# Second experts of a two-block transformer kernel: two accumulation arrays in DRAM, four places for gate and up weights, loops over twelve experts

## The reference, cut to what matters

```python
N_EXPERTS_2 = 64
TOP_K = 6
# per expert e, for the tokens that chose it (rows h of the normalised input):
#   hid = silu(h @ w_exp_gate_2[e]) * (h @ w_exp_up_2[e]) * gate_weight      1024 -> 256
#   out[token] += hid @ w_exp_down_2[e]                                      256 -> 1024
# x = x + gate_m * (shared_expert(h) + sum over experts)
# result: rms_norm(x, g_final_2)
```

## Time and profile before

| | |
|---|---|
| three runs | 1967.75, 1969.74, 1974.19 us, median 1969.74 |
| the profiled execution | 1969.31 us, of which its span is 1967.3 us |
| mean granted TensorE clock in it | 0.960 |
| experts' gate and up products of the second block | from 1248 to 1921 us of the span |
| end of the experts to end of the span | 46 us |

### The profile page before, as it was taken

One profiled execution on the slowest core, in us unless ns is written; L12 is line 12 of the kernel. 1 busy time (PEld: TensorE's weight loads), 2 busy tenths in 40 slices (PEclk: granted clock), 3 DMA queues, 4 the chain that ended last, 5 costly groups with the idle time before them and its releaser, 6 DMA issues. The chain is left out here.

```text
span 1967.3 us, 24773 instructions
## 1 busy us (share of the span) xinstructions
PE 1793.4 (91%) x7962; PEld 1157.1 (59%) x7962; DVE 1007.1 (51%) x1976; ACT 781.6 (40%) x1404; POOL 559.0 (28%) x435
## 2 busy tenths in 40 slices
PE   6989999989989959999999699899999999999992
PEld 3434447754333327776788575577766766666661
DVE  1766416431111136632633344677777776767673
ACT  2411226311110135633632122566655555555551
POOL 4997707011111118901100000222322222222321
PEclk9889999989999979999999799999999999999996
DMA  5353410658999953322022444599999999999973
GB/s 192 129 181 107 171 43 4 253 190 358 407 404 397 359 179 110 106 86 91 1 86 90 163 177 160 186 343 340 348 325 327 333 328 337 329 326 325 320 262 108
DMA packets 116829, 441.71 MB, mean 225 GB/s; under 512 B 27428, under 2 KB 31924, under 8 KB 79368
## 3 DMA queue, kind: packets, MB, share of 16 engines
q1 hardware_dynamic: 93672, 406.94, 54.8%
q0 software_dynamic: 23040, 33.64, 7.4%
q10 hardware_dynamic: 32, 0.04, 0.0%
HBM read 438.34 MB, written 55.11 MB: 251 GB/s over the span
## 5 line engine op out<-in xcount | busy, mean ns | idle before, releaser
L1882 DVE TENSOR_TENSOR big_parts<-big,h_cols_parts 128x1024 fp32r<-128x1024 f32 x256 | 305.7, 1222 | 47.2 <-ACT h_cols_parts L1935 41.2
L2146 POOL DMA_INDIRECT acc_scratch<-heads,small x80 | 131.5, 1644 | 529.4 <-DVE small L1913 296.8
L1935 ACT ACTIVATE h_cols_parts<-big 128x1024 fp32r<-128x1024 f32 x256 | 262.8, 1059 | 27.9 <-PE bank L1841 23.2
L1872 PE MATMUL bank<-big,heads 128*128 128x512 f32 x512 | 235.2, 602 | 0.8 <-ACT heads L1943 0.8
L1839 PE MATMUL bank<-h_cols_parts,heads_parts 128*128 128x512 f32 x512 | 206.2, 403 | 2.2 <-DVE heads_parts L1902 2.2
L1841 PE MATMUL bank<-h_cols_parts,heads_parts 128*128 128x512 f32 x512 | 200.8, 392 | 0.0
L1840 PE MATMUL bank<-big_parts,heads_parts 128*128 128x512 f32 x512 | 200.0, 391 | 0.0
L1872 PEld LDWEIGHTS bank<-big,heads 128*128 128x128 f32 x512 | 92.1, 190 | 92.8 <-issue 91.8
L458 PE MATMUL bank<-big,h_cols 128*128 128x512 f32 x320 | 144.1, 605 | 0.3 <-ACT heads L608 0.3
L1968 ACT ACTIVATE heads<-bank 128x512 f32<-128x512 f32 x64 | 38.3, 598 | 239.5 <-DMA acc_scratch<-heads,small 213.5
L1517 PE MATMUL bank<-big,heads 128*64 128x512 f32 x512 | 118.5, 617 | 14.7 <-DMA big<-in_w_exp_up_dram 13.9
(11 more groups left out here) (438 smaller groups left out, 3335.2 us busy)
## 6 DMA issues: line engine op xcount, KB each, us to landing
big<-in_w_exp_gate_dram SPq DMA_DIRECT2D x96, 1024.0 KB, 13.4
big<-in_w_exp_up_dram SPq DMA_DIRECT2D x96, 1024.0 KB, 20.5
big<-in_w_exp_down_dram SPq DMA_DIRECT2D x72, 1024.0 KB, 22.8
big<-in_w_in_dram SPq DMA_DIRECT2D x13, 2048.0 KB, 8.7
x_res<-in_w_exp_down_dram SPq DMA_DIRECT2D x16, 1024.0 KB, 25.0
junk<-in_w_mod_dram SPq DMA_DIRECT2D x12, 1024.0 KB, 5.1
spare<-in_w_mod_dram SPq DMA_DIRECT2D x12, 1024.0 KB, 6.4
big<-in_w_out_dram SPq DMA_DIRECT2D x4, 2048.0 KB, 9.1
```

Of the source, the lines that this page charges most:

```text
L1872: mm = pe.matmul(b_y[half][:, :], hidt[:, b, P * j:P * j + P], dn[q][:, j, 512 * half:512 * half + 512], start=j == 0, stop=j == FH - 1)
L1882: dve.tensor_tensor(gu_low[q][:, :, part, :], gu[q][:, :, part, :], gu_high[:, :, part, :].bitcast(F32), ALU.subtract).then_inc(w_low, 1)
L1935: act.activation(gu_high[:, :, part, :], gu[q][:, :, part, :], ACT.Copy).then_inc(w_high, 1)
L2146: return pool.indirect_dma_start(out=K.acc_dram, out_offset=bass.IndirectOffsetOnAxis(at, 0), in_=rows, in_offset=None, bounds_check=S - 1 ...
```

## The change

- Even experts' scatters add into an array of their own in DRAM, `even_dram`, odd ones into `acc_dram` as before. Each has its own semaphore. The scatter of expert i-1 waits for that of i-3, not i-2. The waits of ACT and DVE still ask for expert i-3.
- `even_dram` is cleared in `merge`: POOL zeroes a tile and SP writes it out four times, between the last two weight loads.
- Gate and up weights have a fourth place, in `h_rows`. SP's wait for expert e asks for the product of expert e-4 instead of e-3. Since `h_rows` holds the shared expert's result, SP first waits until that is stored; then it loads expert 3.
- Loops go over twelve experts on every engine (4 times; steps 52 to 64 are written out), since 12 is a multiple of 2, 3, 4 and 6.
- After the experts SP loads `even_dram` as four tiles once expert 62 has landed, and DVE multiplies each by the gate vector and adds it to the residual: eight instructions in a chain, before the barrier at the stage's end.

```diff
@@ class ExpertWeights @@
-        self.gu = [as_gate_up(K.big[:, 4096 * q:4096 * q + 4096]) for q in range(3)]
-        self.gu_low = [as_gate_up(K.big_parts[:, 4096 * q:4096 * q + 4096]) for q in range(3)]
+        self.gu, self.gu_low = ([as_gate_up(a[:, 4096 * q:4096 * q + 4096]) for q in range(3)] + [as_gate_up(last)]
+                                for a, last in ((K.big, K.hr.rearrange("p t d -> p (t d)")), (K.big_parts, K.hr_parts[:, :])))
@@ def experts_stage @@
-    *gathered, scattered = K.row_sems[tag]
+    *gathered, last_scattered = K.row_sems[tag]
+    scattered = (K.even_scattered if even else last_scattered, last_scattered)
+    target = (K.even_dram if even else K.acc_dram, K.acc_dram)
...
-        loops = (E - 8) // 6
+        loops = (E - 8) // 12
...
+    def landed(e, b):
+        return (scattered[b], 8 * (e - b) + 16) if even else (last_scattered, 16 * e + 16)
@@ DVE and ACT, step i @@
-                        dve.wait_ge(scattered, 16 * (i - 2))
+                        dve.wait_ge(*landed(i - 3, b))
@@ POOL, step i @@
-                    if late(i, 2):
-                        pool.wait_ge(scattered, 16 * (i - 1))
+                    if even:
+                        if late(i, 3):
+                            pool.wait_ge(*landed(i - 3, b))
+                    elif late(i, 2):
+                        pool.wait_ge(*landed(i - 2, 1 - b))
                     pool.sem_inc(row_dmas, 1)
-                    scatter_add(K, pool, ys[:, b, :], idx[:, q:q + 1]).then_inc(scattered, 16)
+                    scatter_add(pool, target[b], ys[:, b, :], idx[:, q:q + 1]).then_inc(scattered[b], 16)
@@ SP @@
             def both(e, r):
-                sp.wait_ge(au_mm, e - 2)
-                weights.gate_up(sp, e, r % 3)
+                if late(e, 4):
+                    sp.wait_ge(au_mm, e - 3)
+                weights.gate_up(sp, e, r % 4)
                 if late(e, 4):
                     sp.wait_ge(y_mm, e - 3)
                     weights.down(sp, e - 1, (r - 1) % 3)
 
-            loops = (E - 4) // 3
+            for ready, n in init:
+                sp.wait_ge(ready, n)
+            loops = (E - 4) // 12
             both(3, 3)
...
+            if even:
+                sp.wait_ge(*landed(E - 2, 0))
+                for t in range(T):
+                    sp.dma_start(even.rows[t], K.even_dram[P * t:P * t + P, :]).then_inc(even.arrived, 16)
@@ def merge, SP @@
-            load_jobs(K, sp, 6)
+            load_jobs(K, sp, 5)
+            sp.wait_ge(K.pool.sem, K.pool.n)
+            for t in range(T):
+                sp.dma_start(K.even_dram[P * t:P * t + P, :], zeros).then_inc(acc_moved, 16)
+            load_jobs(K, sp, 1)
@@ new, run by DVE after its last step @@
+    def add(self, dve):
+        K = self.K
+        step = K.dve.on(dve)
+        dve.wait_ge(self.arrived, self.n_before + 16 * T)
+        for t in range(T):
+            step(dve.tensor_tensor(self.rows[t], self.rows[t], K.gain[:, :], ALU.mult))
+            step(dve.tensor_tensor(K.x[:, t, :], K.x[:, t, :], self.rows[t], ALU.add))
```

More of the change, by code:

```diff
@@ L1769, in hier_router, with experts_stage @@
     return load, vectors, scalar, vector
-def experts_stage(K, tag, m, weights, init):
+def experts_stage(K, tag, m, weights, init, even=None):
     nc, E = K.nc, m.E
@@ L1879, in low @@
             def low(i, r, k):
-                q, part = (r + 1) % 3, slice(two * k, two * k + two)
+                q, part = (r + 1) % 4, slice(two * k, two * k + two)
                 dve.wait_ge(w_high, PARTS * i + (PARTS + k + 1))
@@ L1924, in step @@
                     if late(i, 3):
-                        dve.wait_ge(scattered, 16 * (i - 2))
+                        dve.wait_ge(*landed(i - 3, b))
                     dve.tensor_copy(ys[:, b, 0:512], b_y[0][:, :]).then_inc(y_dve, 1)
             all_steps(dve, step)
+            if even:
+                even.add(dve)
         @block.scalar
@@ L2006, in both @@
                     weights.down(sp, e - 1, (r - 1) % 3)
-            loops = (E - 4) // 3
+            for ready, n in init:
+                sp.wait_ge(ready, n)
+            loops = (E - 4) // 12
             both(3, 3)
             with sp.Fori(0, loops, 1) as n:
-                for k in range(3):
-                    both(n * 3 + (4 + k), 4 + k)
-            for e in range(4 + 3 * loops, E):
+                for k in range(12):
+                    both(n * 12 + (4 + k), 4 + k)
+            for e in range(4 + 12 * loops, E):
                 both(e, e)
@@ L2997, in shared_expert, with __init__ @@
     return parts
+class EvenExperts:
+    def __init__(self, K):
+        self.K = K
+        self.rows = [a[:, D * n:D * n + D] for a in (K.junk.rearrange("p b d -> p (b d)"), K.spare[:, :]) for n in range(2)]
+        self.arrived, self.n_before = K.acc_moved, 16 * 2 * T
+    def add(self, dve):
[5 more added lines that the diff above has]
+            step(dve.tensor_tensor(K.x[:, t, :], K.x[:, t, :], self.rows[t], ALU.add))
 def second_experts(K):
     m, I = K.m2, K.I
-    experts_stage(K, "moe2", m, K.moe2, [(K.rows_stored, 16 * T), (K.acc_stored, 16 * T)])
+    experts_stage(K, "moe2", m, K.moe2, [(K.rows_stored, 16 * T), (K.acc_stored, 16 * T)], even=EvenExperts(K))
     overflow_stage(K, "moe2", m, I["w_exp_gate_2"], I["w_exp_up_2"], I["w_exp_down_2"])
```

47 lines of the change are left out of this document (29 added, 18 removed).

## The result

The change makes the kernel slower: 1987.73 us (median of three runs, 1985.61 to 1991.04) against 1969.74, a ratio of 1.0094 (95% interval 1.0074 to 1.0114). I had said 1952.0 and at most 1969. The profiled execution has a span of 1986.0 us against 1967.3 before: 18.7 us more.

A forecast was written before the change was run, and what follows sets the result against it. The prediction took the chain of serial scatters (10.67 us an expert) as the bound, with TensorE's 10.21 behind it. From 1969.31 us, -24.8 + 0.5 + 2.0 + 5.0 = -17.3 gave 1952.0, range 1945 to 1969.

The forecast's parts named there:

- the one on the DMA engines: Experts' stage: queues busy 94 to 97% at the new pace, little room left; +0.5 us for occasional late gathers.
- The chain of serial scatters: Experts' stage: each scatter waiting for the last sets 10.67 us an expert; two arrays restore TensorE's 10.21, -24.8 us.
- Rival B: Experts' stage: DMA engines become the bound, not fillable beyond 95%, 10.45 us an expert; 13 us on top, 1965; chance 0.18.
- Fourth place: SP's weight loads: all three go out together behind the down product; counted 0, gathers pushed back only within the range.
- Start: Start of the experts' stage: expert 3's 2 MB load while the uncovered first gather runs; +2 us (0 to 3.5).
- End: End of the experts' stage: loading and adding the even array delays the load of `final`; +5.0 us (3 to 8).
- clearing the even array: SP's four stores between the last two weight loads fit into idle DMA time while TensorE is busy; 0.
- loops of twelve: Experts' loops on every engine: fewer turns, no pause in the present ones; 0 if the code stays in the engines.
- rival D: Experts' loops: the longer body does not stay where instructions are kept; costs 0 to 30 us, 1952 to 1982; chance 0.08.
- Rival C: Experts' stage: two scatters take turns, each over 19.6 us to landing, period stays 10.67; slower, 1976.5; chance 0.10.

The follow-up runs named there:

- a_spread: Changed kernel with each list's tokens put into other slots, so the first 48 lie evenly over the 128 slots; 1957.55 us, ratio to before 0.9939.
- b_spread: The kernel before the change, with tokens spread evenly over the 128 slots of each list; 1932.28 us, ratio to before 0.9821.
- a_two_arrays: Changed kernel with the fourth weight place, loops of twelve and new load order taken back, two arrays and merge kept; 1970.33 us, ratio to before 1.0017.
- a_paced: Changed kernel, SP only: down weights loaded a step earlier, expert 3's load held until the first gather landed; 1967.42 us, ratio to before 0.9997.
- a_four_places: Changed kernel with one array and serial scatters, no clearing or merge; four places, loops of twelve and load order kept; 1981.61 us, ratio to before 1.0075.
- a_halves: Changed kernel with odd experts' token lists beginning at slot 64, even experts' at slot 0; 1957.18 us, ratio to before 0.9936.

## Why the prediction was wrong

**The step that failed** is the one on the DMA engines: "At the new pace that is 94 to 97%. There is room, little of it. I add 0.5 us". I took a mean over 16 engines for the state of each. The fullest ones had no room in before (by the estimate above 10.6 us of packets a period, against TensorE's 10.21), and 93% was the mean of full and less full engines. The 0.5 us stood where the runs show that the period would not fall at all: it went from 10.69 to 10.79, not to 10.21. With the slots spread, 97% is indeed reached and TensorE never waits, so the sum on the mean was right for even engines only.

**The chain of serial scatters (-24.8).** It was there and was removed, as the rows show, but it was not the cause behind itself. A scatter took some 10 us because part of it stood in full engines: 7.6 with the slots spread, 8.6 with the halves alternating. Taken away alone the chain gave 3.3 us, for the weights came late at nearly the same pace. Left in place with balanced engines it costs nothing in the experts. Two limits at one pace are the sign that I missed (the chain at 10.67 us, the fullest engine at some 10.6). The landing time was no constant of the hardware; I used it as one, and read it from the wrong scatters: the 9.8 of the earlier trace rows belongs to the first block and is near the right value by luck.

**Rival B** (the DMA engines become the bound, 0.18, 1965) had the right resource and the wrong measure. It put a ceiling on the mean at 95%; the mean ended at 90.5% and, in a_spread and b_spread, the ceiling was passed. It therefore had no way to come out above the period of before. The 358 GB/s weighed there was passed by the kernel before itself, in the first block:

```profile
490.00:540.00 50.00, 50.00 (x236) 19.65 (x233) 8.78 (x20) 6.34 (x13) 8.92 (x7) 1.00 1.02 407
```

The share of 1.02 also warns that packets can overlap on an engine: these shares are no exact measure of a full one.

**Fourth place (0).** The burst was as described, its cost was not: I left "push gathers back" in the range, but it was the weights themselves. Changed against a_two_arrays: +10.2 us in the experts. Together -3.3 and +10.2 make the +6.9, where my sum had -24.3.

**Start (+2, 0 to 3.5).** Measured +3.5, the upper end. The first gather, issued at 1240.03 with expert 3's load just ahead of it (1239.09), reached TensorE at 1247.50, 7.5 us later instead of 4.6; holding that load back (a_paced) or not having it (a_two_arrays) brought 10.4 and 10.2 us.

**End (+5.0, 3 to 8).** Measured +8.3. Changed kernel, timelines of POOL, SP and DVE:

```profile
1936.81 1.57 POOL L2167 DMA_INDIRECT acc_of_even_experts<-heads,small  x1 [6.67 <-DVE heads L1935]
1941.47 1.56 POOL L2167 DMA_INDIRECT acc_scratch<-heads,small  x1 [3.09 <-DVE heads L1935]
```

```profile
1942.89 0.81 SPq L2037 DMA_DIRECT2D junk<-acc_of_even_experts  x2
1943.74 0.91 SPq L2037 DMA_DIRECT2D spare<-acc_of_even_experts  x2
1963.87 2.58 SPq L3089 DMA_DIRECT2D h_rows<-acc_scratch  x4
```

```profile
1951.68 1.23 DVE L3045 TENSOR_TENSOR junk<-junk,gain 128x1024 f32<-128x1024 f32 x1 [11.08 <-DMA spare<-acc_of_even_experts]
...
1960.50 1.23 DVE L3046 TENSOR_TENSOR x_res<-x_res,spare 128x1024 f32<-128x1024 f32 x1
```

With the last product (L1850) at T = 1931.4, SP issued at T + 11.5 (I had 11.1), the rows were there at T + 20.3 (18.8), and eight instructions took 10.05 us (10.1). From their end at 1961.73 to the load of `final` it was 2.1 us, not 0.3.

That 0.3 was no measurement: it came from taking 6.35 us as the landing time of the last scatter of before, whose landing its trace lacks. a_four_places has the same end, and its trace has the landing (timelines of POOL and SP, and the issue's time to landing):

```profile
1944.36 1.56 POOL L2167 DMA_INDIRECT acc_scratch<-heads,small  x1 [5.48 <-DMA acc_scratch<-heads,small]
1950.95 2.90 SPq L3081 DMA_DIRECT2D h_rows<-acc_scratch  x4
```

```profile
acc_scratch<-heads,small POOLq DMA_INDIRECT x1, 4.6
```

The last scatter landed after 4.6 us, at 1948.96, and the load of `final` came 2.0 us behind it. So the barrier takes about 2 us behind a DMA and behind VectorE's last instruction alike. In before, a landing taken some 1.7 us too late and a barrier taken 1.7 us too short gave the right sum. After the change the scatter is off the path, and the short barrier is left: of the 3.3 us that the end is dearer than the forecast, 1.5 are in the load and 1.8 in the barrier.

**Right:** clearing the even array, and loops of twelve. From the load of `w_o_mla`'s last piece to that of `w_out`'s last piece, with the four stores between them or without, it is 43.5 us in before, changed, a_two_arrays and a_four_places alike. The changed kernel has 8 packets each in q8 and q14 in 600 us where 4 and 3 had been, and a_spread and a_halves, with the same long loops, run at 10.22 us a period with TensorE busy for all of 1300 to 1880 us: rival D is out. **Rival C** (scatters take turns, over 19.6 us to landing) is out too: in a_two_arrays they landed in 11.5 and 11.3 us (the changed kernel's own trace lacks these landings). It named the right sign for a wrong reason.

What stays open is how a burst of three loads makes weights later when the bytes are the same. The share of each single DMA engine was seen only indirectly, through the slot tables and the number of packets in flight.

## What to carry to other kernels

A mean share of the DMA engines below one is room only if the work is spread evenly. Where partitions are partly empty (token lists, masks, tails), ask which engines serve the full ones, and place the rows so that all carry the same over a few periods; here a table of 128 numbers gave 1.8% to the kernel before, more than the whole rebuilding of its scatters could. When a wait's length is a DMA's landing time under load, the removal of the wait proves little: ask first what the landing time is made of, and what would be late next at the same pace. Packets times their duration, added up for the fullest engine, would have given 10.6 us a period before the change was made.

## What was not expected of the hardware

- With mean shares of 0.93, 0.91 and 0.85 the same kernels were short of DMA, and with 0.97 not. 344 GB/s were moved in the last case, 310 in the worst.
- The landing time of a scatter depended on the slots used: some 10.1 us in before against 7.6 in b_spread for the same rows. Without weight traffic the stage's last scatter, of 22 rows, landed in 4.6 us (a_four_places) and in 3.6 (b_spread).
- The end is 24.7 us in before and 17.9 in b_spread. Most of that is the backlog of scatters: the last one is issued 18.0 us behind the last product in before and 12.3 in b_spread.
- Alternating halves between experts was worth as much as spreading every list (1957.18 and 1957.55 us). That fits weights being loaded two or three experts ahead, which would even out what one expert's rows do; the lead was not varied with balanced slots.
